# Two MLPs of 256 tokens: the activation's high part and rest side by side in one moving operand of 512 columns

## What is computed

```
def sq_relu_mlp(h, w1, w2):            # D_MODEL = 1024, D_FF = 4096
    return jnp.square(jax.nn.relu(h @ w1)) @ w2
x = x + g2 * sq_relu_mlp(modulate(rms_norm(x, norm2_g[l]), sh2, sc2), w_mlp1[l], w_mlp2[l])
```

## Time and profile before

| what | value |
|---|---|
| median of 3 runs | 2920.62 us |
| profiled execution | 2921.71 us, span 2919.7 us, granted clock 0.975 |
| TensorE busy | 2746.5 us, 94% of the span |
| VectorE / ScalarE busy | 1635.2 us (56%) / 1147.5 us (39%) |
| chain that ended last | TensorE 87%, VectorE 6%, ScalarE 4% |
| MLP of 256 tokens, first block | from about 939.5 to 1128 us |
| MLP of 256 tokens, second block | from about 2726 to 2914.5 us |

### The profile page before, as it was taken

One profiled execution on the slowest core, in us unless ns is written; L12 is line 12 of the kernel. 1 busy time (PEld: TensorE's weight loads), 2 busy tenths in 40 slices (PEclk: granted clock), 3 DMA queues, 4 the chain that ended last, 5 costly groups with the idle time before them and its releaser, 6 DMA issues.

```text
span 2919.7 us, 43409 instructions
## 1 busy us (share of the span) xinstructions
PE 2746.5 (94%) x16596; PEld 2251.1 (77%) x16596; DVE 1635.2 (56%) x2739; ACT 1147.5 (39%) x2093; POOL 375.6 (13%) x583
## 2 busy tenths in 40 slices
PE   6999899999898997999899999998999998997899
PEld 4646777777747996887688888877777786975899
DVE  4455533334655657885377777773433344378665
ACT  4233422222434445346345455543322234332443
POOL 0000000000000000000176666630000000042000
PEclk9999999999999998999999999999999999998999
DMA  7253244442363543223200000032444423200453
GB/s 280 83 211 154 98 173 172 173 162 87 107 240 132 186 179 139 92 96 112 91 1 1 2 1 1 2 130 87 155 174 172 182 94 126 87 30 15 152 181 143
DMA packets 49612, 343.33 MB, mean 118 GB/s; under 512 B 5296, under 2 KB 7344, under 8 KB 9776
## 3 DMA queue, kind: packets, MB, share of 16 engines
q1 hardware_dynamic: 44960, 324.03, 30.1%
q10 hardware_dynamic: 4496, 17.15, 1.5%
HBM read 333.82 MB, written 7.34 MB: 117 GB/s over the span
## 4 chain that ended last, share of the span: by engine, by line
PE 87%; DVE 6%; ACT 4%; issue 2%; DMA 1%; POOL 0%; DVEq 0%; PEldq 0%; ACTq 0%; PEld 0%; SPq 0%; POOLq 0%
PE ps L540 20%; PE ps L542 19%; PE ps L541 19%; PE ps L1939 4%; PE ps L1926 3%; PE ps L708 3%; PE ps L1918 2%; PE ps L1947 2%; PE ps L763 1%; DMA ring<-in_w_dram 1%; PE ps L568 1%; DVE ring_rest L528 1%; ACT H L514 1%; PE ps L738 1%; PE ps L1881 1%
## 5 line engine op out<-in xcount | busy, mean ns | idle before, releaser
L540 PE MATMUL ps<-hidden_high,w_high 128*128 128x256 f32 (+1 forms) x1160 | 388.4, 335 | 9.8 <-DVE h_rest L536 7.1
L1054 ACT ACTIVATE w_high<-ring 128x2048 fp32r<-128x2048 f32 x124 | 236.9, 1911 | 383.9 <-DMA ring<-in_w_dram 259.3
L540 PE MATMUL ps<-h_high,w_high 128*128 128x512 f32 (+1 forms) x1024 | 351.8, 344 | 16.1 <-DVE h_low L1460 13.6
L541 PE MATMUL ps<-h_low,w_high 128*128 128x512 f32 (+1 forms) x1024 | 347.6, 339 | 0.0
L541 PE MATMUL ps<-hidden_low,w_high 128*128 128x512 f32 (+1 forms) x1024 | 343.5, 335 | 0.0
L1469 DVE TENSOR_TENSOR mix_high<-ring,w_high 128x2048 fp32r<-128x2048 f32 x56 | 128.4, 2292 | 247.3 <-ACT w_high L1054 247.3
L542 PE MATMUL ps<-hidden_high,ring_rest 128*128 128x256 f32 (+1 forms) x872 | 263.7, 302 | 0.0
L2260 POOL TENSOR_SCALAR RS<-C,arena 128x128 f32<-128x128 f32 x128 | 74.9, 604 | 1444.5 <-DVEq L1841 1444.5
L540 PEld LDWEIGHTS ps<-hidden_high,w_high 128*128 128x128 f32 x1160 | 218.6, 188 | 42.9 <-issue 16.6
L540 PEld LDWEIGHTS ps<-h_high,w_high 128*128 128x128 f32 x1024 | 195.8, 191 | 45.1 <-issue 24.8
L1469 DVE TENSOR_TENSOR ring_rest<-ring,w_high 128x2048 fp32r<-128x2048 f32 x68 | 155.9, 2293 | 121.9 <-ACT w_high L1054 121.9
(11 more groups left out here) (404 smaller groups left out, 6015.2 us busy)
## 6 DMA issues: line engine op xcount, KB each, us to landing
ring<-in_w_dram SPq DMA_DIRECT2D x302, 1024.0 KB, 4.9
z_spill<-arena ACTq DMA_DIRECT2D x16, 256.0 KB, 2.0
arena<-z_spill SPq DMA_DIRECT2D x2, 2048.0 KB, 9.4
C<-in_first_dram ACTq DMA_DIRECT2D x1, 2432.0 KB, 10.8
X<-in_x_dram ACTq DMA_DIRECT2D x1, 2048.0 KB, 13.1
x_spill<-X ACTq DMA_DIRECT2D x1, 2048.0 KB, 6.3
X<-x_spill SPq DMA_DIRECT2D x1, 2048.0 KB, 8.2
C<-in_third_dram ACTq DMA_DIRECT2D x1, 2048.0 KB, 8.8
```

Source lines behind the costliest of these rows:

```text
L540: ins = nc.tensor.matmul(out_, w_high, high, start=first, stop=False)
L541: nc.tensor.matmul(out_, w_high, rest, start=False, stop=False)
L1054: nc.scalar.activation(W_HIGH[:, (j + 1) % 2, :], ring[:, s], ACT.Copy).then_inc(sems["w_high"], 1)
```

## The change

For T = 256 the rest of an activation tile is written into columns 256 to 511 of the tile that holds its high part (`rest_of`). `two_products` then issues per piece one product of 512 columns (high weights by high part and rest) and one of 256 (rest of the weights by the high part), instead of three of 256. The two halves of a PSUM bank hold two sums that have yet to be added: ScalarE copies the second half into `RELU` (`second_half`), VectorE adds the first half to it, and then squares it with the ReLU folded in, or adds it with its gate to `X`. The MLPs of 512 tokens stay as they are.

```diff
+        def rest_of(high, low, k, T):
+            return low[:, k, 0:T] if T == T2 else high[:, k, L:T2]
+        def two_products(b, both, w_high, w_rest, k):
+            def wide():
+                return nc.tensor.matmul(ps[:, b, :], w_high, both, start=(k == 0), stop=(k == KD - 1))
+            def narrow():
+                return nc.tensor.matmul(ps[:, b, 0:L], w_rest, both[:, 0:L], start=False, stop=False)
+            return (wide(), narrow()) if k < KD - 1 else (narrow(), wide())
...
+            def second_half(i, n, b):
+                if n < 2:
+                    act.wait_ge(freed[6 + n], i * 2 + v.freed(6 + n, 0))
+                elif n < 10:
+                    act.wait_ge(sems["squared"], i * 16 + v.of("squared", n - 1))
+                else:
+                    last = mlp_bank(n // 2 - 1, n % 2, host)
+                    act.wait_ge(freed[last], i * 2 + v.freed(last, 2))
+                nc.scalar.activation(RELU[:, n % 2, 0:L], ps[:, b, L:T2], ACT.Copy).then_inc(sems["affine"], 1)
...
-                        nc.scalar.activation(RELU[:, n % 2, 0:T], ps[:, b, 0:T], ACT.Relu).then_inc(freed[b], 1)
+                        if T == T2:
+                            nc.scalar.activation(RELU[:, n % 2, :], ps[:, b, :], ACT.Relu).then_inc(freed[b], 1)
+                        else:
+                            second_half(i, n, b)
...
+                    for n in ((2 * j - 8, 2 * j - 7) if j > 3 and T == L else ()):
+                        b = mlp_bank(j, n % 2, host)
+                        act.wait_ge(filled[b], i * mlp_per(b, host) + v.filled(b, mlp_nth(j, host)))
+                        second_half(i, 8 + n, b)
+                        if not more and norm_next:
+                            act.wait_ge(freed[b], i * mlp_per(b, host) + v.freed(b, mlp_nth(j, host) + 1))
+                            act_square(act, v, n, T)
...
+                        r = RELU[:, n % 2, 0:T]
+                        if T == L:
+                            dve.wait_ge(sems["affine"], i * 16 + v.of("affine", n + 1))
+                            nc.vector.tensor_tensor(r, ps[:, b, 0:L], r, ALU.add).then_inc(freed[b], 1)
                         dve.wait_ge(freed[b], i * mlp_per(b, host) + v.freed(b, mlp_nth(j, host) + 1))
...
+                        if T == L:
+                            nc.vector.scalar_tensor_tensor(SQR[:, n % 2, 0:L], r, 0.0, r, ALU.max, ALU.mult).then_inc(sems["squared"], 1)
+                        else:
+                            nc.vector.tensor_tensor(SQR[:, n % 2, 0:T], r, r, ALU.mult).then_inc(sems["squared"], 1)
...
+                            r = RELU[:, n % 2, 0:L]
+                            dve.wait_ge(sems["affine"], i * 16 + v.of("affine", 8 + n + 1))
+                            nc.vector.tensor_tensor(r, ps[:, b, 0:L], r, ALU.add).then_inc(sems["squared"], 1)
+                            dve.wait_ge(sems["squared"], i * 16 + v.of("squared", 8 + n + 1))
+                            at = 2 * (5 * KD + n)
+                            nc.vector.scalar_tensor_tensor(X[:, n, 0:L], r, M[:, at:at + 1], X[:, n, 0:L], ALU.mult, ALU.add).then_inc(freed[b], 1)
```

More of the change, by code:

```diff
@@ L840, in u_mlp @@
             banks_ = {**{b: 12 for b in range(4)}, 4: 8, 5: 8, 6: 6, 7: 6, "slab": 2 * MLP_SLABS + MOD_SLABS} if host else {}
-            return {**U_MLP, **banks_, **(U_SUMS if norm_next else {})}
+            return {**U_MLP, **banks_, **({} if host else {"squared": 2 * HT, "affine": 2 * HT}), **(U_SUMS if norm_next else {})}
         def hosts(n):
@@ L882, in quarter @@
                         ws = slice(k * 256 + t * P, k * 256 + (t + 1) * P)
-                        begun, ins = three_products(ps[:, b, 0:T], high[:, k, 0:T], low[:, k, 0:T], W_HIGH[:, j % 2, ws], mlp_rest(v, j, own, T)[:, ws],
-                                                    k == 0, k == KD - 1)
+                        w_high, w_rest = W_HIGH[:, j % 2, ws], mlp_rest(v, j, own, T)[:, ws]
+                        if T == T2:
+                            begun, ins = three_products(ps[:, b, :], high[:, k, :], low[:, k, :], w_high, w_rest, k == 0, k == KD - 1)
+                        else:
+                            begun, ins = two_products(b, high[:, k, :], w_high, w_rest, k)
                         if t == 0 and k == 0:
@@ L1057, in quarter @@
                         act.wait_ge(filled[b], i * mlp_per(b, host) + v.filled(b, mlp_nth(j, host)))
-                        nc.scalar.activation(RELU[:, n % 2, 0:T], ps[:, b, 0:T], ACT.Relu).then_inc(freed[b], 1)
+                        if T == T2:
+                            nc.scalar.activation(RELU[:, n % 2, :], ps[:, b, :], ACT.Relu).then_inc(freed[b], 1)
+                        else:
+                            second_half(i, n, b)
                         for m in ([n - 1] if n else []) + ([n] if n == 7 else []):
-                            act.wait_ge(sems["squared"], i * 8 + v.of("squared", m + 1))
+                            act.wait_ge(sems["squared"], i * (8 if T == T2 else 16) + v.of("squared", m + 1))
                             nc.scalar.activation(HID_HIGH[:, m, 0:T], SQR[:, m % 2, 0:T], ACT.Copy).then_inc(sems["hidden_high"], 1)
-                    for n in ((2 * j - 8, 2 * j - 7) if j > 3 and not more and norm_next else ()):
+                    for n in ((2 * j - 8, 2 * j - 7) if j > 3 and not more and norm_next and T == T2 else ()):
                         b = mlp_bank(j, n % 2, host)
@@ L1475, in quarter @@
                             dve.wait_ge(sems["hidden_split"], i * 8 + v.of("hidden_split", n - 1))
[L1476 to L1477 removed]
+                        if T == L:
+                            nc.vector.scalar_tensor_tensor(SQR[:, n % 2, 0:L], r, 0.0, r, ALU.max, ALU.mult).then_inc(sems["squared"], 1)
+                        else:
+                            nc.vector.tensor_tensor(SQR[:, n % 2, 0:T], r, r, ALU.mult).then_inc(sems["squared"], 1)
                         for m in ([n - 1] if n else []) + ([n] if n == 7 else []):
                             dve.wait_ge(sems["hidden_high"], i * 8 + v.of("hidden_high", m + 1))
[L1480 removed]
+                            nc.vector.tensor_tensor(rest_of(HID_HIGH, HID_LOW, m, T), SQR[:, m % 2, 0:T], HID_HIGH[:, m, 0:T].bitcast(F32),
                                                     ALU.subtract).then_inc(sems["hidden_split"], 1)
```

6 lines of the change are left out of this document (4 added, 2 removed).

## The result

The changed kernel takes 2928.82 us (median of 10 runs, 2927.69 to 2932.54), the kernel before 2921.77 (10 runs, 2920.09 to 2923.99): ratio 1.0024, 95% interval 1.0016 to 1.0033. It is **7.0 us slower**. The median lies just over the bound of 0.2% that the prediction works with, and the interval reaches to both sides of it. The time is inside my range by 0.2 and 5.5 above my point; 1.2 of these 5.5 are no part of the change: the kernel before took 2920.62 in the three runs that I knew and 2921.77 in ten. The profiled execution took 2930.03 with a span of 2928.1.

A forecast was written before the change was run, and what follows sets the result against it. TensorE was taken to bound the MLPs, with the weights chain just ahead. Its 12.0 us product gain, less longer chains and ends, gave +3.1 and -0.4 in the two MLPs, +2.7: median 2923.3 us, range 2914.5 to 2929.0.

The forecast's parts named there:

- my +2.7: Whole kernel: first MLP +3.1 us and second -0.4, together 2.7 slower, within the 0.2% that can't be told from none.
- Three narrow ones are 357.6 ns, a wide and a narrow one 345.9: TensorE in the 256-token MLPs: 11.7 ns saved per piece, 0.187 us per slab, 12.0 us in all.
- not near 346: Sign of being wrong: start spacing of a wide and narrow pair in the two MLPs is not near 346 ns.
- the pair doesn't get cheaper: Rival: in the MLPs wide plus narrow still costs 357.6 ns; +10.4 us, 2931.0; chance 0.06.
- Slab 5 starts at 23.55: Looped quarter: slab 5 starts 23.55 us after slab 0's end, against 22.89 before, so this half gets 0.66 longer.
- slab 5's wait, 0.9: Each quarter: TensorE waits about 0.9 us for slab 5's rest of the weights; under 0.4 or over 1.5 means wrong.
- shorter by 0.08: First MLP: a quarter takes 45.69 us, 0.08 less than before (0.24 less in the second MLP).
- 5.43 per slab against 5.53, it keeps pace: Up part, after slab 2: the chain feeding the weights takes 5.43 us per slab, TensorE 5.53; 0.10 to spare.
- the rival of the longer chain: Rival: chain of 5.55 us exceeds the slab, every up-part slab waits, slab 5 by 1.35; +7.7 us, 2928.3; chance 0.15.
- The last quarter of the first MLP: Slabs 6 and 7's weights stand behind the normalisation's squares on ScalarE; 2.50 us lost, slab 6 at 7.16 after slab 5.
- the tail I had at +0.88: Behind either MLP's last product: copy and addition come before the gate with nothing to hide them, +0.88 us.
- VectorE is far from full, so its work as such costs nothing: Both MLPs: added VectorE work is free; the cost comes where ScalarE waits for the square and weights wait behind it.

The follow-up runs named there:

- the changed kernel's third profile: The changed kernel run once more without any edit, a single profile to look at TensorE's granted clock, which did not fall: 2927.14 us, span 2925.1.

## Why the prediction was right, and where it was off

The sign of my +2.7, the places and the mechanism were right; the size was 4.3 too small, and that put the result at the edge of the 0.2%, to the slower side of which I gave 24%. That the time is still inside my range, by 0.2, is luck.

**"Three narrow ones are 357.6 ns, a wide and a narrow one 345.9": the step that failed.** The pair costs 351.1. I carried the wide product's price over from rows in which the rest of the weights lies in another buffer. The trace of the kernel before has both cases in one and the same MLP of 512 tokens; 24 products lie between the first row and the second, and between the third and the fourth:

```profile
400.21 0.39 PE L542 MATMUL ps<-hidden_high,mix_high 128*128 128x512 f32 x1
...
405.65 0.39 PE L542 MATMUL ps<-hidden_high,mix_high 128*128 128x512 f32 x1
...
444.69 0.39 PE L542 MATMUL ps<-h_high,ring_rest 128*128 128x512 f32 x1
...
450.28 0.40 PE L542 MATMUL ps<-h_high,ring_rest 128*128 128x512 f32 x1
```

5.44 against 5.59: 226.7 ns where the rest of the weights is a tile of its own (`mix_high`, slabs 1 to 7 of the 512-token MLPs), 232.9 where it stands in place over the ring (`ring_rest`, slab 0 there, `mlp_rest` in the kernel). This holds throughout that trace: in the 11 stretches of wide products with `ring_rest` the mean spacing is 231.1 to 232.9, in the 44 with `mix_high` 226.7 to 227.7. Busier engines are not what sets them apart, as one slab of either kind shows (columns as in the earlier trace rows):

```profile
445.00:455.00 10.00, 10.00 (x45) 8.06 (x44) 2.75 (x5) 1.23 (x2) 0.00 (x0) 1.00 0.32 105
458.00:467.00 9.00, 9.00 (x41) 7.48 (x40) 3.49 (x3) 2.92 (x3) 0.00 (x0) 1.00 0.52 218
```

(VectorE 28% and ScalarE 12% busy in a slab with `ring_rest`, 39% and 32% in one with `mix_high`.) The MLPs of 256 tokens have `ring_rest` in every slab. With 232.6 for the wide product, the mean of most of these stretches, a wide and a narrow one would have been 351.8, close to the 351.1 that came. The whole gain is then 1024 x 6.6 ns = 6.8 in place of 12.0, 0.106 per slab in place of 0.187. This is the mark I had set for being wrong ("not near 346"), about halfway to the rival "the pair doesn't get cheaper". The page "TensorE: Matmul & The Clock Gate" of the Trainium skill, section "Back-to-back issue gap", gives a formula for the gap of an isolated product by which 2.5 ns per piece would be saved; the trace shows 6.6, and neither of its two sizes (109.2 and 215.8 ns against 117.6 and 233.5), so it comes nearer to the saving than I did with both of its sizes off.

**"Slab 5 starts at 23.55": right,** with errors that cancel. The end of slab 0, from which I counted, is here slab 1's start, 996.73. Slab 2 starts 6.04 after it, forecast 6.04, and slab 5 at 1020.18 - 996.73 = 23.45. The rest of slab 2's weights ends at 5.80 (forecast 5.79), though the chained square is 0.07 shorter: the first addition starts at 0.34 where the square started at 0.26. At slab 4 I had the chain run by itself; in the trace the copy of its last tile waits for TensorE, and TensorE's slabs are dearer:

```profile
1014.25 0.39 ACT L1070 ACTIVATE arena<-ps 128x256 f32<-128x256 f32 x1 [2.11 <-PE ps L551]
```

So the addition of tile 7 stands at 17.94 and not at 17.78, and the rest of slab 5's weights ends at 23.40 (forecast 23.30); TensorE then starts 0.05 behind it, where I took 0.25. What I called slab 5's wait, 0.9, is 0.5 by starts, because TensorE, with dearer pairs, gets there later; by its bracket, 0.35, it would be under the 0.4 that I had named as a sign of being wrong. Slabs 5, 6, 7 and 0 take 22.59, forecast 22.14: 4 x 0.085 of it is the pair, 0.1 that slab 5 lasts 5.7 (as before the change, 5.78 against 5.71). The quarter then takes 46.04, forecast 45.69; "shorter by 0.08" became longer by 0.27.

**"5.43 per slab against 5.53, it keeps pace": right,** with more room (slabs of 5.62): slabs 3 and 4 don't wait, and the rival of the longer chain falls, though its price, +7.7, is near the result. A time alone would not have told the two apart; the places of the waits do.

**The last quarter of the first MLP: right.** From slab 5 to slab 6 it takes 1119.22 - 1112.01 = 7.21 (forecast 7.16), from there to slab 7 7.55 (7.55). To the sums of the normalisation it is 22.67 (1134.68 - 1112.01), against 19.08 before (1128.13 - 1109.05, the start of slab 5's first product): +3.6, forecast 2.50 + 0.88. TensorE's wait for these sums is the tail I had at +0.88; it went from 1.12 to 2.06:

```profile
1132.50 0.43 PE L475 MATMUL ps<-RS,ones 128*32 128x64 f32 x16 [2.06 <-ACT RS L455]
```

This row is of the changed kernel's third profile; in its first the wait is 2.06 as well. The kernel with pairs in the first three quarters alone fits this share: +0.5 of the 6.5.

**The sum again.** With 351.1 ns for the pair and 0.42 for the chained square the same walk gives about +4.3 for both MLPs together. The profiles without a fall of the clock show +4.3 and +1.4 in the two stages (198.3 - 193.97, 194.1 - 192.74), 1.4 more than the walk. The fall, where it occurs, adds 1.5 in the first (199.78 against 198.3), of which 0.1 to 0.2 is the longer wait itself; it was no term of my sum. So of the 4.3 by which +2.7 was short of +7.0, 1.6 are the prices of pair and square, about 1.5 are starts later than walked (slab 5 at 23.45 where the shorter square would put it near 23.3; the second MLP's quarters another 0.2 longer, at 46.25), and the rest, 1.2, can be the clock in those executions in which it falls, or chance in the medians. A part of the later starts is the copy that waits for TensorE's dearer slabs, above; the 0.2 of the second MLP is not explained, and the kernel with the added steps alone, whose slabs are not dearer, missed its walk by 1 in the same direction.

**"VectorE is far from full, so its work as such costs nothing": right.** The kernel with additions in the slack slabs is faster than before; the kernel with a quarter of the additions, in slabs 0 and 3, is slower, at 1.0018.

What stays open: the price of a wide product goes with the buffer that holds the rest of its stage's weights (232.6 against 226.7 in the kernel before), and the load of the engines is ruled out; but no run moved that buffer alone, and why it matters is not shown. Nor is it shown why the wide product steps by 233.5 in turn with narrow ones, 231 grouped and 230.5 with only wide ones. Whether without the clock's fall the ratio would be below 1.002 was not measured.

## What to carry to other kernels

Take the price of a product from rows with the operands it will have: 7 ns on one of 227 was nearly half the gain here, and rows with the same rest of the weights, 45 us further on in the same trace, had it. A whole-slab mean is better than one difference of two rows. When a change trades TensorE's time for a step on another engine, ask slab by slab whether that step stands ahead of something the next slab needs; the same edit was worth -4.0 in the slabs with slack and +4.8 in those without. So apply it where the slack is, and leave the tight slabs and the stage's end as they are.

## What the hardware showed that I had not expected

The granted clock of TensorE fell from 1.00 to 0.50 for some 3.4 us shortly after a wait, at 950.6 in the changed kernel, whose wait ended at 949.52, in the four profiles of twelve with the longest waits (1.78 to 2.06), and in none of the eight others (1.53 to 1.74). The wait's length varies between executions of one kernel by up to 0.24, and the same program's clock fell in one execution and not in another, at a price of about 1.5. Wide products step by 232.6 ns where the rest of the weights stands over the ring and by 226.7 where it has a tile of its own, in one kernel and even in one MLP. A scalar_tensor_tensor of 128x256 whose operands are all in SBUF and are one tile takes 425 ns, as long as an addition out of PSUM (421), and 485 where it reads M and X.
